# Attention heads taken in pairs, and rotary rows exchanged by transfers within SBUF

## The chip, the cores and the metric

The kernel runs on one core of a Trainium2 chip. The metric is the time of one execution in microseconds (us) on the device; of several executions the median is given. TensorE is written PE, its weight loads PEld, VectorE DVE, ScalarE ACT, GpSimd POOL and SyncE SP.

## The reference

Two transformer stacks of two layers each are applied to 256 positions of width 1024, in fp32. Most of the arithmetic is dense projections: feed-forward layers of hidden width 2816, input and output projections of the mixers, and a cross attention. Four self-attentions of eight heads of 64 stand among them. Cut to what the change touches:

```python
# A: forgetting attention      s = q @ k.T / 8 + cum_logf[q] - cum_logf[k], causal
# B: differential attention    4 heads of two maps each, rotary q and k, chunk mask:
#    p = softmax(s0) - lam * softmax(s1);  out = p @ v          (v is 128 wide)
# D: chunk band attention      s = q @ k.T / 8 + rel_table[clip(q - k)], chunk mask
# E: dilated attention         rotary q and k, log(count of patterns) as bias
rot = concat([x1 * cos - x2 * sin, x2 * cos + x1 * sin])   # x1, x2: dims 0..7 and 8..15 of a head
p = softmax(where(allowed, s, -inf));  out = p @ v
```

## The kernel before

All activations lie transposed: 128 features on the partitions, 256 positions along the row. A dense product is split into high and low fp32r parts (`hi*hi`, `lo*hi`, `hi*lo`), so one *unit* of weights (8 blocks of 128x128, or 4 for half of a row range) is 24 (or 12) matmuls of 128x256 on PE, lines 598, 599, 602 or 616 to 618. `plan_stream` lists all units in order. Weights come by SP into a ring of four buffers `raw`; ACT copies a unit to `w_hi` (line 984) and DVE subtracts to `w_lo` (line 1376), each when PE has finished the unit that held the slot before, up to four units ahead. PE, ACT, DVE and POOL each run the same written-out program `order`, in which every stage takes lists of units ("between") as filler, so that PE has dense work while the attention's softmax runs on ACT and DVE. `take` on PE is the matmuls of a unit, on ACT the split of a later unit into `w_hi`, on DVE the evacuation of the unit's PSUM bank (one of four, `acc`) and the split into `w_lo`.

One attention (`attend`) runs in 11 steps over 8 heads. In step i PE computes the scores of head i (lines 707, 708; contraction over 64 partitions; causal blocks only, so 384 columns in PSUM bank `wide[:, i % 2]`), turns the probabilities of head i-2 (line 717: three 128x128 transposes), multiplies head i-3 by its values (lines 727, 728; 64 output rows, the partition half of the head), and then takes the step's filler. DVE adds the bias and finds the row maximum (`biased`), and scales the probabilities of the head before (`probs`); ACT takes the exponential and its sum (line 1133) and copies the turned probabilities to SBUF (line 1141); DVE copies a finished pair of heads out (line 1625). fp32 matmuls are recorded as two passes each.

Ahead of B and E `rotate` forms, on PE, the rotary partner of every row by a permutation matrix (line 688, four matmuls of 128x512); DVE reads it from PSUM and makes `x*cos + partner*sin` by three instructions for each pair of blocks (lines 1574, 1576, 1577: a *spin*, four of them). The first two spins are needed for the first scores. Ahead of D `band_bias` reads the relative bias of each head by a skewed transfer, mirrors it by a reversal matrix on PE (line 824) and adds the mask on DVE (lines 1724, 1725). The same `rotate` with another matrix serves the retention after E, and is not changed.

Of the kernel before, what the change touches and what calls it, by code (L numbers as in the profile page):

```python
# [15 lines left out]
P = 128  # L16
# [36 lines left out]
class Counts:  # L53


    def __init__(self):
        self.norm = 0
        self.gen = 0
        self.fill = 0
        self.head = 0  # L60
        self.rot = 0
        self.att = 0
        self.pv = 0
        self.group = 0
        self.conv = 0
# [115 lines left out]
def build(nc, io, out):  # L181
# [22 lines left out]
    with ExitStack() as ctx:  # L204
# [24 lines left out]
        silu_g = sb("silu_g", [P, 2, T])  # L229
        hidf = sb("hidf", [P, 2, T])  # L230
# [8 lines left out]
        ident, ones, ones64, perm_rope, perm_ret = (mats[:, i, :] for i in range(5))  # L239
        reverse = mats[:, 6, :]  # L240
# [19 lines left out]
        rot_done, rot_added = sem("rot_done"), sem("rot_added")  # L260
# [23 lines left out]
        band_in, band_turned, band_masked = sem("band_in"), sem("band_turned"), sem("band_masked")  # L284
# [33 lines left out]
        def band(h):  # L318
            return work[:, 8 + 2 * h:10 + 2 * h, :] if h < 4 else keep[:, 8 + 2 * (h - 4):10 + 2 * (h - 4), :]
# [3 lines left out]
        def gate_bias(h):  # L323
            if h < 5:
                return flat(work[:, 8:16, :])[:, TRI * h:TRI * h + TRI]
            return flat(keep[:, 4:8, :])[:, TRI * (h - 5):TRI * (h - 4)] if h < 7 else lower(hidf)

        def slot_prob(g):
            return lower(prob[:, g % 3, :, :])

        def slot_turned(n):
            return lower(probT[:, n % 2, :, :])
# [5 lines left out]
        def attention(kind):  # L338

            def halves(v, b0):

                return [(h, [(v[:, :, 64 * h:64 * h + 64], 0, 64 * (h % 2))], [b0 + h // 2] if h % 2 else []) for h in range(8)]

            if kind == "A":
                return ([(half(16, h), half(20, h), gate_bias(h), None) for h in range(8)], halves(vals(32, 4), 0), 0.125)
            if kind == "B":
                v = vals(36, 4)
                return ([(half(24, i), half(28, i), chunked, i - 1 if i % 2 else None) for i in range(8)],  # L350
                        [(2 * h + 1, [(v[:, :, P * h:P * h + P], 0, 0)], [4 + h]) for h in range(4)], 0.125)
            if kind == "D":
                return ([(half(16, h), half(20, h), lower(band(h)), None) for h in range(8)], halves(vals(36, 4), 4), 0.125)
# [1690 lines left out]
```

## Time and profile before

| | |
|---|---|
| median of 3 executions | 2274.04 us (2272.51 to 2276.78) |
| the profiled execution | 2286.41 us, of which its span 2284.3 |
| PE busy | 2208.1 us (97%) |
| DVE busy | 1521.3 us (67%) |
| ACT busy | 1184.3 us (52%) |
| mean granted PE clock | 0.989 |

The span runs from the first to the last instruction. Busy time of PE is that of pipelined matmuls whose ends are modelled, so two records overlap and the distance between starts is what a matmul costs. The four attentions lie at 276 to 328 (A), 348 to 405 (B, with its rotation), 961 to 1024 (D, with its band) and 1492 to 1563 us (E, with its rotation).

### The profile page before, as it was taken

What the parts mean: (1) busy time and instruction counts of PE and PEld (TensorE: products, weight loads), DVE (VectorE), ACT (ScalarE), POOL (GpSimd) and SP (SyncE); (2) the same over time, 40 slices, a digit from 0 to 9 for tenths busy, and PEclk for the clock granted to TensorE, in tenths of its full rate; (3) what the DMA queues carried; (4) which work ended last, traced back from release to release, by engine and by line L of the source; (5) the groups of instructions that cost most, each with busy time, mean ns of one, the idle gap of its engine ahead of it and who ended that gap; (6) DMA issues with size and microseconds to landing.
All of it is one profiled execution on the core that took longest, in us unless ns stands there. A gap on an engine that the chain in (4) does not pass through costs nothing.

```text
span 2284.3 us, 45071 instructions
## 1 busy us (share of the span) xinstructions
PE 2208.1 (97%) x18355; PEld 2145.9 (94%) x18355; DVE 1521.3 (67%) x2344; ACT 1184.3 (52%) x1852; POOL 122.7 (5%) x146
## 2 busy tenths in 40 slices
PE   5999998899999999999999999999999999989998
PEld 5999987899999999888999999988999999989998
DVE  5766657676666666666766666677766666667664
ACT  5644453665456544446654554535654554556543
POOL 2001000110011001001100000100100000101001
PEclk9999998999999999999999999999999999999999
DMA  7555532356565657423665665642765665635653
GB/s 240 179 180 175 165 120 65 111 177 206 181 194 168 209 180 236 156 80 106 207 199 188 198 188 192 220 142 86 224 194 187 195 202 183 188 101 180 191 193 102
DMA packets 383756, 393.29 MB, mean 172 GB/s; under 512 B 6897, under 2 KB 381809, under 8 KB 383425
## 3 DMA queue, kind: packets, MB, share of 16 engines
q1 hardware_dynamic: 381632, 383.30, 52.7%
q0 software_dynamic: 1920, 7.11, 1.1%
q8 instruction: 148, 2.42, 0.5%
q14 instruction: 56, 0.45, 0.1%
HBM read 389.34 MB, written 1.05 MB: 171 GB/s over the span
## 4 chain that ended last, share of the span: by engine, by line
PE 86%; DVE 6%; ACT 4%; issue 2%; POOL 1%; DMA 1%; SPq 0%; POOLq 0%; DVEq 0%; ACTq 0%
PE acc L598 24%; PE acc L599 24%; PE acc L602 24%; DVE w_lo L1376 2%; ACT w_hi L984 2%; PE acc L616 2%; PE acc L617 2%; PE acc L618 2%; PE acc L567 1%; PE acc L569 1%; PE acc L568 1%; POOL t L1883 1%; PE wide L727 1%; DMA raw<-in_ffn_w_in 1%; PE wide L782 1%
## 5 line engine op out<-in xcount | busy, mean ns | idle before, releaser
L1376 DVE TENSOR_TENSOR w_lo<-raw,w_hi 128x1024 fp32r<-128x1024 f32 (+2 forms) x790 | 897.8, 1139 | 503.7 <-ACT w_hi L984 501.3
L984 ACT ACTIVATE w_hi<-raw 128x1024 fp32r<-128x1024 f32 (+2 forms) x790 | 776.3, 988 | 806.6 <-PE acc L602 739.4
L598 PE MATMUL acc<-hn_hi,w_hi 128*128 128x256 f32 x3328 | 792.7, 280 | 25.3 <-DMA colc<-in_cols 18.1
L599 PE MATMUL acc<-hn_lo,w_hi 128*128 128x256 f32 x3328 | 786.3, 278 | 0.0
L598 PEld LDWEIGHTS acc<-hn_hi,w_hi 128*128 128x128 f32 x3328 | 628.9, 189 | 30.6 <-DMA colc<-in_cols 18.1
L599 PEld LDWEIGHTS acc<-hn_lo,w_hi 128*128 128x128 f32 x3328 | 629.1, 189 | 0.9 <-issue 0.8
L602 PE MATMUL acc<-hn_hi,w_lo 128*128 128x256 f32 x3328 | 449.6, 278 | 0.0
L602 PEld LDWEIGHTS acc<-hn_hi,w_lo 128*128 128x128 f32 x3328 | 412.6, 188 | 0.0
L599 PE MATMUL acc<-hid_lo,w_hi 128*128 128x256 f32 x1408 | 331.6, 277 | 0.0
L598 PE MATMUL acc<-hid_hi,w_hi 128*128 128x256 f32 x1408 | 331.5, 277 | 0.0
L599 PEld LDWEIGHTS acc<-hid_lo,w_hi 128*128 128x128 f32 x1408 | 264.8, 188 | 0.0
L598 PEld LDWEIGHTS acc<-hid_hi,w_hi 128*128 128x128 f32 x1408 | 264.7, 188 | 0.0
L1883 POOL TENSOR_TENSOR t<-t 128x256 f32<-128x256 f32 x119 | 107.8, 906 | 2152.5 <-ACT t L1026 2105.8
L602 PE MATMUL acc<-hid_hi,w_lo 128*128 128x256 f32 x1408 | 192.4, 277 | 0.0
L602 PEld LDWEIGHTS acc<-hid_hi,w_lo 128*128 128x128 f32 x1408 | 175.2, 188 | 0.0
L598 PE MATMUL acc<-mn_hi,w_hi 128*128 128x256 f32 x512 | 132.6, 295 | 4.2 <-DVE mn_lo L1478 4.2
L599 PE MATMUL acc<-mn_lo,w_hi 128*128 128x256 f32 x512 | 126.9, 283 | 0.0
L598 PEld LDWEIGHTS acc<-mn_hi,w_hi 128*128 128x128 f32 x512 | 99.3, 194 | 7.7 <-issue 7.2
L1511 DVE TENSOR_TENSOR silu_g<-acc,rstd 128x256 f32<-128x256 f32 x176 | 74.4, 423 | 40.8 <-PE acc L602 28.0
L599 PEld LDWEIGHTS acc<-mn_lo,w_hi 128*128 128x128 f32 x512 | 99.3, 194 | 0.9 <-issue 0.7
L1520 DVE TENSOR_TENSOR hidf<-silu_g,acc 128x256 f32<-128x256 f32 x176 | 73.8, 420 | 28.7 <-PE acc L602 27.0
L1430 DVE SCALAR_TENSOR_TENSOR hn_lo<-x,gains,hn_hi 128x256 fp32r<-128x256 f32 x112 | 82.1, 738 | 8.9 <-ACT hn_hi L1022 8.9
(255 smaller groups left out, 2261.5 us busy)
## 6 DMA issues: line engine op xcount, KB each, us to landing
raw<-in_ffn_w_in SPq DMA_DIRECT2D x88, 1024.0 KB, 5.1
raw<-in_ffn_w_out SPq DMA_DIRECT2D x32, 1024.0 KB, 5.2
raw<-in_ffn_pre_w_gate SPq DMA_DIRECT2D x22, 1024.0 KB, 5.4
raw<-in_ffn_pre_w_up SPq DMA_DIRECT2D x22, 1024.0 KB, 5.3
raw<-in_ffn_post_w_gate SPq DMA_DIRECT2D x22, 1024.0 KB, 5.3
raw<-in_ffn_post_w_up SPq DMA_DIRECT2D x22, 1024.0 KB, 5.4
raw<-in_x_w_kv SPq DMA_DIRECT2D x16, 1024.0 KB, 5.5
raw<-in_ffn_pre_w_down SPq DMA_DIRECT2D x16, 1024.0 KB, 5.1
```

The costliest lines, as they stand in the source:

```text
L598: nc.tensor.matmul(bank, wh[:, j, :], a_hi[:, u.k0 + j, :], start=u.first and j == 0, stop=False)
L599: nc.tensor.matmul(bank, wh[:, j, :], a_lo[:, u.k0 + j, :], start=False, stop=False)
L602: mm = nc.tensor.matmul(bank, wl[:, j, :], a_hi[:, u.k0 + j, :], start=False, stop=u.last and j == u.nk - 1)
L616: nc.tensor.matmul(bank, ah, wh, start=j == 0, stop=False)
L617: nc.tensor.matmul(bank, ah, wl, start=False, stop=False)
L618: mm = nc.tensor.matmul(bank, al, wh, start=False, stop=j == u.nk - 1)
L984: nc.scalar.activation(w_hi[:, u.slot, 0:u.nk, :], raw[:, u.raw % RING, 0:u.nk, P * u.half:P * u.half + P], ACT.Copy).then_inc(w_hi_ready, 1)
L1376: nc.vector.tensor_tensor(w_lo[:, u.slot, 0:u.nk, :], raw[:, u.raw % RING, 0:u.nk, P * u.half:P * u.half + P], w_hi[:, u.slot, 0:u.nk, :]. ...
L1430: nc.vector.scalar_tensor_tensor(hn_lo[:, k, :], x[:, k, :], gains[:, gain + k:gain + k + 1], hn_hi[:, k, :].bitcast(F32), ALU.mult, ALU.s ...
L1511: nc.vector.tensor_tensor(silu_g[:, h, :], out_ap(units[u0 + h].out), rstd[:, 0, :], ALU.mult)\
L1520: nc.vector.tensor_tensor(hidf[:, h, :], silu_g[:, h, :], out_ap(units[u0 + 2 + h].out), ALU.mult).then_inc(hid_mul, 1)
L1883: nc.gpsimd.tensor_tensor(t1[:, 0, :], t1[:, 0, :], t1[:, k, :], ALU.add).then_inc(squares_added, 1)
```

## The change

Heads are taken two by two. `attend` has five steps instead of eleven. In step m, PE issues the first score matmul of both heads of pair m, then the second of both; head 0 lies on partitions 0 to 63, head 1 on 64 to 127, and their scores go to banks 0 and 1 of `wide`. Then follow filler, the transposes of head 0 of pair m-1, filler, the transposes of head 1, filler, and the values of both heads of pair m-1, which write partitions 0 to 63 and 64 to 127 of one bank. DVE makes one instruction for the bias of a pair (128x768) and two for its scaling; ACT's exponentials stay four for a pair. In B only the second of two maps is turned, and its values are 128 wide, so no two of them stand side by side there.

The permutation matmuls ahead of B and E go. ACT issues eight transfers (four of 8x1536 and four of 8x512 elements) that exchange rows 0 to 7 and 8 to 15 of each half into `prob` and `probT`, after its last split, and DVE's spins wait for all of them and read SBUF instead of PSUM; the sign is in the sine table. The band of D is laid out whole on the host, comes by two transfers instead of eight, and gets its mask by four DVE instructions of 128x768, which stand between the projections of D; line 824 goes. The deal of filler units over the steps is rewritten.

```diff
@@ order
-                    att("A", spread(memk[5:8] + span("bq", "bk")))
+                    att("A", deal(memk[5:8] + span("bq", "bk"), 1, 1, 1, 1, 1, 0, 1, 1, 0, 1, 1, 0, 1, 1, 0))
...
-                    rotate(work[:, 24:32, :], perm_rope, rope_c, rope_s, memv[2:4])
-                    att("B", [memv[4:6], memv[6:8], [(0, 4)], half[0:1], half[1:2], half[2:3], half[3:4], [], [], [], []])
-                    head(cat[:, 4:8, :], 4, 128, ["subln"] * 4, half[4:6], half[6:8])
+                    rope(work[:, 24:32, :], rope_c, rope_s, memv[2:4])
+                    att("B", [[memv[4:6], memv[6:8], [(0, 4)]], [half[0:1], half[1:2], []], [half[2:3], [], []],
+                              [half[3:4], [], []], [half[4:5], [], []]])
+                    head(cat[:, 4:8, :], 4, 128, ["subln"] * 4, half[5:6], half[6:8])
...
-                    att("D", [memv[0:2], memv[2:4], memv[4:6], memv[6:8] + [(0, 4)], half[0:1], half[1:2], half[2:3], half[3:4],
-                              half[4:5], half[5:6], half[6:8]], final=True)
+                    att("D", [[memv[0:2], memv[2:4], []], [memv[4:6], memv[6:8], [(0, 4)]], [half[0:1], half[1:2], half[2:3]],
+                              [half[3:4], half[4:5], half[5:6]], [half[6:7], half[7:8], []]], final=True)
...
-                    rotate(work[:, 28:36, :], perm_rope, dil_c, dil_sn, span("ev"))
-                    att("E", spread(span("rq", "rk", "rg")), final=True)
+                    rope(work[:, 28:36, :], dil_c, dil_sn, span("ev"))
+                    att("E", deal(span("rq", "rk", "rg"), 1, 1, 1, 1, 1, 0, 1, 1, 0, 1, 1, 0, 1, 1, 1), final=True)
@@ PE, attend
+                def score(m):
+                    if kind in "BE" and m < 2:
+                        pe.wait_ge(rot_added, c.rot - 2 + 2 * m)
+                    if m:
+                        pe.wait_ge(biased, c.att + 2 * m)
+                    for j, (q, k) in enumerate(heads(m)):
+                        nc.tensor.matmul(wide[:, j, 0:P], q[:, 0:P], k[:, 0:P], start=True, stop=True)
+                    for j, (q, k) in enumerate(heads(m)):
+                        nc.tensor.matmul(wide[:, j, P:TRI], q[:, P:T], k, start=True, stop=True).then_inc(scores, 1)
...
+                def weigh(m):
+                    vs = values(m)
+                    n, size = len(vs) * m, P // len(vs)
+                    pe.wait_ge(turned_copied, c.pv + n + len(vs))
...
+                for m in range(5):
+                    if m < 4:
+                        score(m)
+                    take(between[m][0])
+                    if m and kind != "B":
+                        turn(m - 1, 0, 2 * m - 2)
+                    take(between[m][1])
+                    if m and kind != "B":
+                        turn(m - 1, 1, 2 * m - 1)
+                    elif m:
+                        turn(m - 1, 1, m - 1)
+                    take(between[m][2])
+                    if m:
+                        weigh(m - 1)
@@ ACT, attend
+                for m in range(5):
+                    take(between[m][0])
+                    if m and kind != "B":
+                        copy_turned(2 * m - 2)
+                    if m < 4:
+                        exponent(m)
+                    take(between[m][1])
+                    if m:
+                        copy_turned(per * m - 1)
+                    take(between[m][2])
...
@@ ACT, rope
+                for b, home in ((0, rope_first), (6, rope_last)):
+                    for p0 in (0, 64):
+                        for to, at in ((p0, p0 + 8), (p0 + 8, p0)):
+                            act.dma_start(home[to:to + 8], src[at:at + 8, b:b + (2 if b else 6), :]).then_inc(rot_in, 16)
+                take(between)
@@ DVE, rope and attend
+                dve.wait_ge(rot_in, 128 * (c.rope + 1))
+                for b in (0, 2, 1, 3):
+                    home = rope_first[:, 2 * b:2 * b + 2, :] if b < 3 else rope_last
+                    spin(src[:, 2 * b:2 * b + 2, :], t1[:, 2 * b:2 * b + 2, :], home, cs, sn)
...
+                for m in range(5):
+                    if m and kind != "B":
+                        normalise(m - 1)
+                    if m < 4:
+                        bias(m)
+                    if m and kind == "B":
+                        normalise(m - 1)
+                    take(between[m][0])
+                    take(between[m][1])
+                    take(between[m][2])
+                    if m:
+                        copy_out(m - 1)
```

The order of the instructions shows the same in two places. The first is PE in the middle of A, from the end of one filler unit to the start of the next; before it reads

```order
L602 MATMUL acc<-hn_hi,w_lo 128x256 x8
L707 MATMUL wide<-work 128x128
L708 MATMUL wide<-work 128x256
L717 MATMUL wide<-mats,prob 128x128 x3
L727 MATMUL wide<-probT,work 64x256
L728 MATMUL wide<-probT,work 64x128
```

and of the changed kernel (line 620 is the end of a unit, 729 the transposes, 740 and 742 the values, 719 and 721 the scores)

```order
L620 MATMUL acc<-hn_hi,w_lo 128x256 x8
L729 MATMUL wide<-mats,prob 128x128 x3
L740 MATMUL wide<-probT,work 64x256 x2
L742 MATMUL wide<-probT,work 64x128 x2
L719 MATMUL wide<-work 128x128 x2
L721 MATMUL wide<-work 128x256 x2
```

Values and scores of two heads now stand together, and the values of a pair follow the transposes of its second head with no unit between. The second place is ACT in the same stretch, two steps of before and one of after (line 984, then 1002, is the split of a weight unit, 1133, then 1149, the exponential, 1141, then 1157, the copy of turned probabilities):

```order
L1133 ACTIVATE prob,small<-prob,small 128x128
L1133 ACTIVATE prob,small<-prob,small 128x256
L1141 ACTIVATE probT<-wide 128x384
L984 ACTIVATE w_hi<-raw 128x1024
L1133 ACTIVATE prob,small<-prob,small 128x128
L1133 ACTIVATE prob,small<-prob,small 128x256
L1141 ACTIVATE probT<-wide 128x384
L984 ACTIVATE w_hi<-raw 128x1024
```

```order
L1002 ACTIVATE w_hi<-raw 128x1024
L1157 ACTIVATE probT<-wide 128x384
L1149 ACTIVATE prob,small<-prob,small 128x128
L1149 ACTIVATE prob,small<-prob,small 128x256
L1149 ACTIVATE prob,small<-prob,small 128x128
L1149 ACTIVATE prob,small<-prob,small 128x256
L1002 ACTIVATE w_hi<-raw 128x1024
L1157 ACTIVATE probT<-wide 128x384
```

The copy that the values wait for stood ahead of the split, and stands behind it now.

## Rows read from the trace of the kernel before

**Rows 1.** Page, its heading and part 1: busy us, share of span, instructions.
```profile
span 2284.3 us, 45071 instructions
PE 2208.1 (97%) x18355; PEld 2145.9 (94%) x18355; DVE 1521.3 (67%) x2344; ACT 1184.3 (52%) x1852; POOL 122.7 (5%) x146
```
**Rows 2.** Stretches A, B, D, E: length, busy us by engine, clock, DMA share, GB/s.
```profile
276.40:328.10 51.70, 49.41 (x356) 41.52 (x356) 34.85 (x77) 22.11 (x51) 0.00 (x0) 1.00 0.41 123
348.00:404.50 56.50, 48.47 (x287) 41.23 (x286) 41.03 (x97) 20.81 (x54) 0.00 (x0) 0.82 0.21 66
961.20:1024.00 62.80, 58.65 (x395) 47.84 (x394) 42.23 (x109) 25.05 (x64) 0.00 (x0) 1.00 0.23 71
1492.40:1562.80 70.40, 67.27 (x483) 57.03 (x482) 50.31 (x102) 28.96 (x61) 0.00 (x0) 1.00 0.33 107
```
**Rows 3.** Timeline of PE around A: start us, us, line, operation, shape, count.
```profile
270.10 1.07 PE L602 MATMUL acc<-mn_hi,w_lo 128*128 128x256 f32 x8
272.82 1.07 PE L602 MATMUL acc<-mn_hi,w_lo 128*128 128x256 f32 x8
...
276.54 0.48 PE L707 MATMUL wide<-work 64*128 64x128 f32 x2
...
280.32 0.48 PE L707 MATMUL wide<-work 64*128 64x128 f32 x2
...
305.74 0.48 PE L707 MATMUL wide<-work 64*128 64x128 f32 x2
...
306.59 0.55 PE L717 MATMUL wide<-mats,prob 128*128 128x128 f32 x3
...
310.80 0.49 PE L707 MATMUL wide<-work 64*128 64x128 f32 x2
```
**Rows 4.** Timeline of PE in the last mixer: matmuls on halves of the array.
```profile
2016.11 1.98 PE L895 MATMUL wide<-work 128*64 128x64 f32 x32
...
2038.26 1.13 PE L909 MATMUL wide<-work,t 64*128 64x256 f32 x6
```
**Rows 5.** Timeline of ACT in A, split and copy behind one unit.
```profile
320.29 1.06 ACT L984 ACTIVATE w_hi<-raw 128x1024 fp32r<-128x1024 f32 x1 [2.83 <-PE acc L602]
321.26 0.47 ACT L1141 ACTIVATE probT<-wide 128x384 f32<-128x384 f32 x1
```
**Rows 6.** Groups of DVE by shape: count, busy us, mean ns, idle before.
```profile
L1376 DVE TENSOR_TENSOR w_lo<-raw,w_hi 128x768 fp32r<-128x768 f32 x64 | 61.2, 956 | 67.3 <-ACT w_hi L984 66.7
```
**Rows 7.** Timeline of PE at the band of D.
```profile
961.21 2.74 PE L824 MATMUL wide<-work,mats 128*128 128x384 f32 x8
...
968.07 0.48 PE L707 MATMUL wide<-work 64*128 64x128 f32 x2 [0.85 <-DVE keep L1725]
```
**Rows 8.** Timelines of PE, ACT and DVE at the rotation of B.
```profile
348.12 3.60 PE L688 MATMUL wide<-work,mats 128*128 128x512 f32 x8
...
357.29 0.49 PE L707 MATMUL wide<-work 64*128 64x128 f32 x2
...
348.38 2.00 ACT L984 ACTIVATE w_hi<-raw 128x1024 fp32r<-128x1024 f32 x2 [3.65 <-PE acc L618]
...
351.75 0.68 DVE L1574 TENSOR_TENSOR t<-wide,keep 128x512 f32<-128x512 f32 x1
...
353.67 0.68 DVE L1574 TENSOR_TENSOR t<-wide,keep 128x512 f32<-128x512 f32 x1
```
**Rows 9.** Timeline of DVE at the rotation of E.
```profile
1495.05 0.68 DVE L1574 TENSOR_TENSOR t<-wide,work 128x512 f32<-128x512 f32 x1
```
**Rows 10.** One issue on SP; then issues of transfers: KB each, us to landing.
```profile
2015.65 0.37 SPq L544 DMA_DIRECT2D raw<-in_gla_w_in  x1
...
keep<-in_band POOLq DMA_DIRECT2D x4, 256.0 KB, 9.5
out<-t SPq DMA_DIRECT2D x4, 256.0 KB, 2.1
```
**Rows 11.** Stretch in B: length, busy us by engine, clock, DMA share, GB/s.
```profile
370.00:380.00 10.00, 6.53 (x34) 5.15 (x32) 7.62 (x22) 5.24 (x16) 0.00 (x0) 0.67 0.16 54
```

More of the change, by code:

```diff
@@ L338, in attention, with heads, values @@
         def attention(kind):
[L342 to L353, printed above, removed]
-            return ([(half(28, h), half(32, h), dil_bias, None) for h in range(8)], halves(vals(40, 4), 0), 0.125)
+            q0, k0, bias, v, out0 = {"A": (16, 20, gate_pair, vals(32, 4), 0), "B": (24, 28, lambda m: both(chunked), vals(36, 4), 4),
+                                     "D": (16, 20, band_pair, vals(36, 4), 4), "E": (28, 32, lambda m: both(dil_bias), vals(40, 4), 0)}[kind]
+            def heads(m):
+                return [(half(q0, 2 * m + j), half(k0, 2 * m + j)) for j in range(2)]
+            def values(m):
+                return [v[:, :, P * m:P * m + P]] if kind == "B" else [v[:, :, P * m + 64 * j:P * m + 64 * j + 64] for j in range(2)]
+            return heads, bias, values, out0
         def order(s):
@@ L816, in gate_biases @@
                         mm.then_inc(gates_spread, 1)
-            def band_bias(c):
-                pe.wait_ge(band_in, 16 * 9)
-                pe.wait_ge(head_std, c.head)
-                for h in range(8):
-                    if h >= 4:
-                        pe.wait_ge(band_masked, h - 3)
-                    nc.tensor.matmul(wide[:, h % 4, 0:TRI], reverse, lower(band(h)), start=True, stop=True)\
-                        .then_inc(band_turned, 1)
-                pe.wait_ge(band_masked, 8)
             def retention(c, half):
@@ L1562, in head_norm, with spin @@
                 take(after)
[L1564 to L1568 removed]
+            def spin(pair, turned_pair, shifted, cs, sn):
+                nc.vector.tensor_tensor(turned_pair, shifted, sn.to_broadcast([P, 2, T]), ALU.mult)
+                link(nc.vector.tensor_tensor(pair, pair, cs.to_broadcast([P, 2, T]), ALU.mult))
+                nc.vector.tensor_tensor(pair, pair, turned_pair, ALU.add).then_inc(rot_added, 1)
@@ L1911, in residual @@
                     pool.dma_start(work[:, 40:42, :], io["masks"][:, 2:4, :]).then_inc(band_in, 16)
-                    for h in range(8):
-                        b = io["band"]
-                        skew = bass.AP(b.tensor, 512 * h, [[1, P], [P, 2], [1, T]])
-                        pool.dma_start(band(h), skew).then_inc(band_in, 16)
+                    pool.dma_start(work[:, 8:14, :], io["band"][:, 0:6, :]).then_inc(band_in, 16)
+                    pool.dma_start(keep[:, 8:14, :], io["band"][:, 6:12, :]).then_inc(band_in, 16)
                 if name == "down4":
```

322 lines of the change are left out of this document (150 added, 172 removed).

## The prediction

> **What bounds the kernel now.** I read the page's busy times first, then the four stretches that hold the attentions, then the order of time inside them. PE is busy for 97% of the span [rows 1]; it runs its program in order, so a microsecond of PE work that goes is a microsecond of time, unless PE then waits. In A, D and E PE is busy 49.4 of 51.7, 58.7 of 62.8 and 67.3 of 70.4 us at full clock; DVE has 35 to 50 us there and ACT 22 to 29 [rows 2]. B is different: PE has 48.5 of 56.5 us at a mean clock of 0.82, DVE 41.2 [rows 2]; it waits on a chain of short instructions, and its clock falls to half where PE has run thin (6.5 of 10 us busy, 0.67 granted, [rows 11]). So the change is worth PE time in A, D and E, and chain length in B.
>
> **What a head costs PE.** A unit of 24 matmuls is 2.72 us (272.82 - 270.10, [rows 3]); a half unit 1.36. Scores alone cost 280.32 - 276.54 - 2.72 = 1.06. Scores, transposes and values of one step cost 310.80 - 305.74 - 2.72 = 2.34 [rows 3], so a pair costs 4.7.
>
> **What a pair will cost PE.** Do two halves of the array run side by side? Line 909 has three matmuls of 64 rows, the first two on different halves, six passes. It ends after 1.13 us [rows 4]; a pass of 256 columns is 2 cycles a column, 0.21 us by my estimate from two unit matmuls of 0.113 (2.72/24), so six in a row with a tail of 0.4 would be 1.5 and four 1.1. So row halves run together. For column halves line 895 doesn't decide: 32 passes of 64 columns in 1.98 us [rows 4] are 0.05 to 0.06 each, which 32 in a row would also give. For the values of a pair I bound: 1.0 us (together) to 1.7 (in a row); I take 1.1. With both together a pair costs one step of a head, 2.34, and a second set of transposes, at most 0.55 [rows 3], 0.45 taken: 2.8 instead of 4.7, so 1.9 less for each of 12 pairs in A, D and E.
>
> The Trainium skill (TensorE: Matmul & The Clock Gate, part 3 on packing small matmuls) gives 3.07 times for four row tiles and 2.38 times for three column tiles, not four and three. An estimate from that page for two tiles is 1.6 times: 0.25 us more on each of 16 score pairs and 12 value pairs, 7 us, and the sum below would be 13 instead of 20.
>
> **The new wait.** In A and E most steps have two units and nothing between the second transposes and the values. Before, ACT copied a head turned in one step for values in the next. Now the copy comes behind the split of the second unit: the row of before has the copy done 1.44 after the split began (321.26 + 0.47 - 320.29, [rows 5]); with an estimated 0.25 from a unit's end to ACT's start that is 1.69 after the unit. The transposes take 0.35 of that, so PE waits 1.35 a pair. Queued behind the values are the scores of the next pair, so all wait. A step of A is then 2 x 2.72 + 2.34 + 0.45 + 1.35 = 9.6, against 2 x 5.06 = 10.1. Does DVE keep up? The bias of a pair is 768 columns, 0.96 by a subtraction of that width [rows 6], or 1.25 ns a column; the maxima of 256 and 512 add 1.0; scaling a pair is 1.2 by the same rate. Three times 1.6 for units and their evacuation make it 5.8 to 7.4 in a step, less than 9.6. ACT has four exponentials (1.8), two copies and two splits, 4.8.
>
> **A.** First step 1.06 + 3 x 2.72 = 9.2; three of 9.6; last without scores 8.6; together 46.6. Before, 276.5 to 328.1 [rows 2, 3]. Less 0.4 for the columns: gain 4.5.
>
> **D.** The band goes: 968.07 - 961.21 = 6.9 us of PE and wait [rows 7]. Its four DVE masks of 768 (1 us each, by [rows 6]) lie between projections, whose unit of 2.72 asks DVE for 1.6; nothing is late there as PE has units split ahead. First step 1.06 + 4 units = 11.9; the second 2.0 + 10.9 + 0.8 + a wait of 1.4 = 15.2. In the third and fourth PE has 7.0 only, and DVE sets the pace: copy out, high and low part of the pair before (1.5), scaling 1.2, bias 2.0, then ACT's exponentials, split and copy 2.9, the values 1.0: 9.0 and 8.4. Last 6.8, and 0.6 for the last block's low part. Together 51.9 against 62.8 [rows 2]: gain 10.9, less 0.4.
>
> **B and its rotation.** Before, ACT ended its split at 350.4 (348.38 + 2.0), DVE began the spins at 351.75, two spins (1.92 each) later PE scored at 357.29 [rows 8]; meanwhile PE had 3.6 us of rotation and two units. Now ACT must issue eight transfers. An issue on SP lasts 0.37 [rows 10], so eight take 3.0; the landing I take as 2.1, as for the smallest load of the listed rows. Nothing in the trace goes from SBUF to SBUF or is issued by ACT: bounds 1 us (everything hidden behind DVE's own split) and 9.5 + 8 x 0.7 = 15, that of the band's transfers on POOL [rows 10] (an issue estimated at twice SP's). I take 5.1, as both are plain hardware transfers. Spins start at 355.4, 3.7 later; scores at 359.3, 2.0 later than before, with PE idle for 5.8 us since it has no rotation. A hole of 3.5 us has lowered the clock here before [rows 11], so I charge 3 more. Against it the chain: a pair is one bias, one maximum, one scaling where two stood, 6.5 us a step instead of two of 4.3, and one unit fewer stands behind it: 6 saved. Net gain 1, between -4 and +6.
>
> The Trainium skill (DMA: Bandwidth & Descriptors, where the 2 us goes) puts the sequencer's dispatch at about 50 ns. By that eight issues would be 0.4, not 3.0, the spins 2.6 earlier in B and E, and the sum 25. The trace's 0.37 stands against it for SP; no row has ACT.
>
> **E.** Spins start 3.8 later than 1495.05 [rows 9]: 1498.8. Four spins 7.7, then four evacuations and splits of 1.55, then bias 2.0: 1514.7. PE has done its four units long before, waits for a bank until 1507, and comes to its second scores at 1515.3. The step after it is 12.6, since DVE holds three units' work ahead of the scaling; two of 9.6; the last 10.0; 0.7 until the last pair is copied: 1557.8 against 1562.8 [rows 2]. Gain 5.0, less 0.4.
>
> **Sum.** 4.5 + 10.5 + 1 + 4.6 = 20.6; say 20. It comes off the profiled execution's 2286.4 (span 2284.3, [rows 1]): 2266. That execution lies 12 above the median of 2274.0; taken off the median: 2254.
>
> **Rivals.**
> 1. *The waits don't come*: copies and transfers hide. Then all PE work counts: 12 x 1.9 = 22.8, four score pairs in B 4.2, band 6.9, two rotations about 3.4 each: 40.7, so 2233. For it: PE is 97% busy [rows 1]. Against it: the copy has 1.35 us behind a split that can't start earlier, and PE has nothing between.
> 2. *The exchange is late*, 10 us instead of 5. B and E each lose 5, and the longer hole costs B 2.5 more at half clock: gain 8, so 2266. For it: one semaphore counts eight transfers and weight loads use the same engines.
> 3. *Halves run in turn.* The change then doesn't do what it says: a score pair costs 1.7 (+0.64 x 16), a value pair 1.7 (+0.6 x 12): 17 less, gain 3: 2271. Against it: line 909 for rows; the columns are open.
> 4. *Slower*: the exchange takes over 15 us from its first issue, as POOL's transfers of the band would. Every microsecond beyond 5 is paid in B and in E, as PE has but two units (B) and four banks (E) to work on meanwhile. Break-even is 5 + 20/2 = 15; at 17 it is 2278.
>
> **How the numbers follow.** Forecast 0.58 (its own range 2246 to 2262), rival 1 0.15, rival 2 0.15, rival 3 0.07, rival 4 0.05. Below 2238 lies half of rival 1, above 2268 rivals 3 and 4: left out about 0.2, so 2238 to 2268. What a measurement can tell from no change is 0.2%, 4.5 us. Faster than 2269.5: forecast, rival 1, rival 2 but for a small part, 0.87; same 0.08; slower 0.05.
>
> **What would show it.** Right: in the changed trace the two score matmuls of a pair start within a few hundredths of a microsecond; the values wait for ACT's copy some 1.3 us in most steps of A and E; PE idles 5 to 6 us ahead of B's first scores with the transfers as releaser; no reversal in D. Wrong: if that hole is under 2 us, the issues are cheap and rival 1 gains; if the second value matmul starts a pass later than the first, the columns run in turn; if DVE's evacuations hold PE in A, my step there is too short. The forecast fails if the exchange takes over 10 us or if D, the largest term, gains under 6.

## The result, and the profile after

Two timings of the changed kernel are on record, each beside runs of the kernel before.

| timing | changed kernel, median (runs) | kernel before, median (runs) | ratio, 95% interval |
|---|---|---|---|
| first | 2266.32 us (7: 2255.11 to 2273.31) | 2276.78 us (7: 2272.51 to 2285.90) | 0.995 [0.9927, 0.9972] |
| second, the same kernel again | 2263.07 us (6: 2259.30 to 2268.36) | 2279.82 us (11: 2275.99 to 2285.60) | 0.9925 [0.9909, 0.9941] |

The change is faster, by 10.5 us in the first timing and 16.8 in the second; forecast were 2254 and a gain of 20. The time lies in the outer range (2238 to 2268), though above the forecast's own (2246 to 2262); the direction is right, the size is short. The page of the changed kernel, its heading and its first part [rows 1]:

```profile
span 2253.3 us, 44894 instructions
PE 2153.0 (96%) x18323; PEld 2110.6 (94%) x18323; DVE 1512.0 (67%) x2244; ACT 1183.1 (53%) x1852; POOL 117.5 (5%) x140
```

The two profiled executions differ by 31.0 us of span, PE's busy time by 55. That is more than either timing gives, so the stages have to be read apart. Below is each attention with what stands around it, of before and then of after: from the first matmul of the head norm ahead of it (D, A), or from the norm of the residual ahead of the projections (E), to the first landmark behind it that both kernels share (A and B: the next head norm; D: the cross attention; E: the first retention scores). Columns as in [rows 2]: stretch, length, busy us of PE, PEld, DVE, ACT, POOL, granted clock, DMA share, GB/s.

```profile
264.80:333.35 68.55, 66.26 (x482) 56.45 (x481) 43.38 (x92) 33.23 (x59) 0.00 (x0) 1.00 0.43 128
333.35:404.50 71.15, 63.12 (x390) 53.97 (x389) 50.52 (x113) 29.99 (x61) 0.00 (x0) 0.86 0.21 69
946.85:1042.05 95.20, 89.65 (x642) 76.76 (x641) 66.43 (x150) 48.11 (x97) 5.93 (x7) 1.00 0.35 113
1475.30:1577.25 101.95, 98.78 (x736) 86.58 (x735) 73.34 (x136) 44.86 (x89) 0.05 (x1) 1.00 0.41 135
```

```profile
258.90:322.50 63.60, 58.31 (x483) 52.58 (x482) 41.60 (x68) 32.70 (x59) 0.00 (x0) 1.00 0.48 148
322.50:392.45 69.95, 53.68 (x382) 47.50 (x381) 48.91 (x98) 29.80 (x62) 0.00 (x0) 0.93 0.21 65
927.00:1012.10 85.10, 76.27 (x626) 69.71 (x625) 59.90 (x110) 47.72 (x97) 5.94 (x7) 1.00 0.39 125
1444.10:1546.20 102.10, 88.81 (x728) 82.50 (x728) 71.67 (x112) 44.65 (x89) 0.06 (x1) 0.97 0.43 139
```

A, B and D became 4.95, 1.2 and 10.1 us shorter (forecast 4.5, 1 and 10.5). E became 0.15 longer, where 4.6 were forecast: PE has 10 us less to do in it and idles for all of them. The four together are 16.1 us.

Most of the other 15 us between the two profiles does not come from the change. A unit of 24 dense matmuls takes either 2.72 or 2.83 us, at a granted clock of 1.00 in both. In the execution of before, the feed-forward after the first norm (some 86 to 260 us) and the one from 711 to 935 us run at the slower pace; in that of after, neither does. The last matmul group of two units in a row, PE's timeline of before, then of after:

```profile
122.17 1.11 PE L602 MATMUL acc<-hn_hi,w_lo 128*128 128x256 f32 x8
125.00 1.11 PE L602 MATMUL acc<-hn_hi,w_lo 128*128 128x256 f32 x8
```

```profile
120.85 1.07 PE L620 MATMUL acc<-hn_hi,w_lo 128*128 128x256 f32 x8
123.57 1.07 PE L620 MATMUL acc<-hn_hi,w_lo 128*128 128x256 f32 x8
```

The starts are 2.83 apart in the one and 2.72 in the other. Over the 14 profiles of this case (both kernels and twelve runs below) the first of these stretches is slow in eight and the second in nine, whichever kernel runs; five other dense stretches that I sampled never are. They account for 4.7 and some 7 us of the 31. If timed runs change pace in the same way, that is up to 12 of the 18 us between the fastest and the slowest run of the first timing.

Now E. The rows are the end of the split on ACT and the issues (ACTq is ACT's queue, the second number the time of all four issues), the first rotation on DVE, and on PE the first scores, the unit behind them, the second scores and the first work behind the attention:

```profile
1461.64 1.06 ACT L1002 ACTIVATE w_hi<-raw 128x1024 fp32r<-128x1024 f32 x1 [1.66 <-PE acc L620]
1462.09 2.84 ACTq L1308 DMA_DIRECT2D prob<-work  x4
1464.96 2.61 ACTq L1308 DMA_DIRECT2D probT<-work  x4
```

```profile
1471.97 0.69 DVE L1604 TENSOR_TENSOR t<-prob,work 128x512 f32<-128x512 f32 x1 [8.01 <-DMA probT<-work]
```

```profile
1476.07 0.51 PE L719 MATMUL wide<-work 64*128 64x128 f32 x4 [3.65 <-DVE work L1606]
...
1480.23 0.58 PE L616 MATMUL acc<-hn_hi,w_hi 128*128 128x256 f32 x1 [2.80 <-DVE work L1452]
...
1490.00 0.49 PE L719 MATMUL wide<-work 64*128 64x128 f32 x4
...
1531.44 3.67 PE L706 MATMUL wide<-work,mats 128*128 128x512 f32 x8 [2.09 <-DVE keep L1659]
```

Eight issues take 5.5 us, 0.65 to 0.71 each; DVE goes on 4.4 us after the end of the last (1471.97 - 1467.57). From its first issue the exchange takes 1471.97 - 1462.09 = 9.9 us (9.3 from the end of the split, 1462.70). In B it takes 345.50 - 337.66 = 7.8 from its first issue, of which 2.0 lie behind the last, and there PE waits 6.55 for the first scores:

```profile
337.66 1.23 ACTq L1308 DMA_DIRECT2D prob<-work  x1
...
338.91 1.96 ACTq L1308 DMA_DIRECT2D prob<-work  x3
340.90 2.61 ACTq L1308 DMA_DIRECT2D probT<-work  x4
```

```profile
345.50 0.69 DVE L1604 TENSOR_TENSOR t<-prob,keep 128x512 f32<-128x512 f32 x1 [4.56 <-DMA probT<-work]
```

```profile
349.60 0.80 PE L719 MATMUL wide<-work 64*128 64x128 f32 x4 [6.55 <-DVE work L1606]
```

The hole in E lowers the clock as well. PE stands still for 3.65 and for 2.80 us, and from 1476.4 to 1483.2 the granted clock is 0.50, the lower of its two levels (1.2 GHz). The matmuls of the first unit in it start 0.213 us apart and not 0.113, which costs some 1.3 us. In all seven profiles with eight transfers the clock falls at this place, for 6.8 us (10.2 in one); in the seven others it does not fall there.

Last, a step of A, on PE and on ACT: after the first two pairs' scores, the step's second unit ends with L620, and the values (L740, L742) and scores (L719, L721) of a pair stand behind the second transposes (L729).

```profile
270.61 0.49 PE L719 MATMUL wide<-work 64*128 64x128 f32 x4
...
279.83 0.49 PE L719 MATMUL wide<-work 64*128 64x128 f32 x4
...
295.31 1.08 PE L620 MATMUL acc<-hn_hi,w_lo 128*128 128x256 f32 x8
296.22 0.49 PE L729 MATMUL wide<-mats,prob 128*128 128x128 f32 x3
297.97 0.65 PE L740 MATMUL wide<-probT,work 128*64 128x256 f32 x4 [1.26 <-ACT probT L1157]
298.45 0.39 PE L742 MATMUL wide<-probT,work 128*64 128x128 f32 x4
298.77 0.49 PE L719 MATMUL wide<-work 64*128 64x128 f32 x4
```

```profile
296.49 1.05 ACT L1002 ACTIVATE w_hi<-raw 128x1024 fp32r<-128x1024 f32 x1
297.44 0.47 ACT L1157 ACTIVATE probT<-wide 128x384 f32<-128x384 f32 x1
```

PE waits 1.26 us for a copy that stands behind a split, as [rows 5] let expect. The starts of the first two pairs' scores in A are 279.83 - 270.61 = 9.22 apart, with three units of 2.72 between, so the scores of a pair take 1.06. The values of a pair take 298.77 - 297.97 = 0.80 us for eight passes; the two matmuls that stand on different halves start 0.007 us apart, for values (column halves) as for scores (row halves).

### The profile page after: what moved, and what is told of

The parts are those of the page before. It is cut to its first block, busy times and chain, and to the rows that moved or that the text cites. A ratio compares the mean times of both kernels' runs of the same rounds, so it can differ in the third digit from the quotient of the medians.

```text
span 2253.3 us, 44894 instructions
## 1 busy us (share of the span) xinstructions
PE 2153.0 (96%) x18323; PEld 2110.6 (94%) x18323; DVE 1512.0 (67%) x2244; ACT 1183.1 (53%) x1852; POOL 117.5 (5%) x140
## 4 chain that ended last, share of the span: by engine, by line
PE 82%; DVE 7%; ACT 5%; issue 3%; DMA 1%; POOL 1%; ACTq 0%; SPq 0%; POOLq 0%; DVEq 0%
PE acc L616 24%; PE acc L620 23%; PE acc L617 23%; DVE w_lo L1415 2%; ACT w_hi L1002 2%; PE acc L634 2%; PE acc L636 1%; PE acc L635 1%; PE acc L585 1%; PE acc L587 1%; PE acc L586 1%; POOL t L1932 1%; ACT prob L1149 1%; DMA raw<-in_ffn_w_in 1%; DVE hn_lo L1469 1%
## 5 line engine op out<-in xcount | busy, mean ns | idle before, releaser
L620 PE MATMUL acc<-hn_hi,w_lo 128*128 128x256 f32 x3328 | 447.3, 277 | 0.0
L620 PEld LDWEIGHTS acc<-hn_hi,w_lo 128*128 128x128 f32 x3328 | 410.5, 188 | 0.0
L620 PE MATMUL acc<-hid_hi,w_lo 128*128 128x256 f32 x1408 | 190.9, 276 | 0.0
L620 PEld LDWEIGHTS acc<-hid_hi,w_lo 128*128 128x128 f32 x1408 | 173.9, 188 | 0.0
L1550 DVE TENSOR_TENSOR gates_hid<-acc,rstd 128x256 f32<-128x256 f32 x176 | 74.4, 423 | 38.5 <-PE acc L620 27.0
L1559 DVE TENSOR_TENSOR gates_hid<-gates_hid,acc 128x256 f32<-128x256 f32 x176 | 73.9, 420 | 26.7 <-PE acc L620 26.1
```

Source lines behind the costliest of these rows:

```text
L620: mm = nc.tensor.matmul(bank, wl[:, j, :], a_hi[:, u.k0 + j, :], start=False, stop=u.last and j == u.nk - 1)
L1550: nc.vector.tensor_tensor(silu_g[:, h, :], out_ap(units[u0 + h].out), rstd[:, 0, :], ALU.mult)\
L1559: nc.vector.tensor_tensor(hidf[:, h, :], silu_g[:, h, :], out_ap(units[u0 + 2 + h].out), ALU.mult).then_inc(hid_mul, 1)
```

## The experiments

**Theory:** the pairs and the band bring what was worked out (16 us in A, B and D); E lost its gain to an exchange that takes 9 us and not 5; what the first timing lacks beside that is the pace of the dense stretches. **Rivals:** E lost it to the pairs themselves (DVE's wider operations); or the change brings only the 10.5 us of the first timing, and something outside the attentions takes the rest. A third shows in the traces, the clock: where the mean granted clock of a stage differs between two runs, its length is no measure of waits alone, and this is said below where it matters.

Stage lengths of all profiles, by the same landmarks (us), and the timed ratios to before:

| kernel | A | B | D | E | ratio, 95% interval |
|---|---|---|---|---|---|
| before | 68.5 | 71.1 | 95.2 | 101.9 | |
| changed | 63.6 | 70.0 | 85.1 | 102.1 | 0.995 [0.9927, 0.9972] |
| changed, again | 63.7 | 70.0 | 85.2 | 101.7 | 0.9925 [0.9909, 0.9941] |
| permutation matmuls | 63.7 | 67.9 | 85.0 | 99.1 | 0.9894 [0.9878, 0.9911] |
| copy before split | 60.5 | 73.7 | 86.6 | 102.0 | 0.9911 [0.9893, 0.9929] |
| two semaphores | 63.7 | 71.4 | 85.0 | 100.1 | 0.9923 [0.9901, 0.9944] |
| unit behind each turn | 70.4 | 70.0 | 84.2 | 107.0 | 0.9993 [0.9975, 1.0012] |
| the same, permutation matmuls | 70.6 | 68.1 | 84.3 | 101.5 | 0.9939 [0.9918, 0.9961] |
| band alone | 68.7 | 70.9 | 88.4 | 103.2 | 0.9944 [0.9926, 0.9961] |
| exchange alone | 68.5 | 77.4 | 95.2 | 108.3 | 1.0043 [1.0024, 1.0062] |
| two transfers | 63.7 | 66.3 | 85.1 | 97.1 | 0.9873 [0.9843, 0.9904] |
| scaling between units | 63.3 | 70.0 | 83.8 | 103.9 | 0.994 [0.9916, 0.9963] |
| all together | 61.7 | 68.4 | 83.8 | 97.4 | 0.9876 [0.9842, 0.9909] |
| split before exponentials | 59.4 | 67.3 | 83.8 | 94.3 | 0.987 [0.9844, 0.9896] |

### The changed kernel again

> The changed kernel once more, unaltered. Theory: its trace gains 5.0 us in A, 1.2 in B, 10.1 in D and loses 0.2 in E, 16 in all; the rest of the 31 us between the two profiled executions is dense stretches in which a unit of before took 2.83 us instead of 2.72, at the same granted clock, which come and go. Then the ratio to before is near 0.993 (0.991 to 0.995) and the landmarks of the attentions come out within 0.5 us of the first profile. Rival: the change really gains 10.5 as the first timing says, 0.9953, and some stage outside the attentions loses 5.

0.9925, and every stage within 0.5 us of the first profile. The stages' 16 us (0.993) lie inside this interval, and at the edge of the first. The rival's 0.9953 lies outside the second. The mean of the two timings, some 14 us, is the best single figure for the change.

### Permutation matmuls for both embeddings

```
             def rope(c, src, cs, sn, between):    # PE
-                take(between)
+                rotate(c, src, cs, sn, between, perm_rope)
             def rope(c, src, cs, sn, between):    # ACT
-                ... eight act.dma_start(home[...], src[...]).then_inc(rot_in, 16)
                 take(between)
             def rope(c, src, cs, sn, between):    # DVE
-                dve.wait_ge(rot_in, 128 * (c.rope + 1))
+                dve.wait_ge(rot_done, c.rot + n + 1)   # per pair, from PSUM
```

> Pairs of heads and the laid-out band stay; both rotary embeddings get their rows by permutation matmuls again. Theory (the exchange is what was mis-sized): the spins of E start 8 us earlier after the stage begins, those of B 4.6 earlier, PE has 3.5 us more of work in each; E becomes 5 to 7 us shorter than in the changed kernel, B 3 to 5, in all 8 to 12, so some 2256 where the changed kernel has 2266. Rival (E lost its gain to the pairs themselves, for instance to DVE's wider operations): E stays within 2 us of the changed kernel and the total moves by less than 3.

2257.1 us against 2263.1 for the changed kernel beside it: 6 us, where 8 to 12 were expected. E is 2.5 to 3 shorter (expected 5 to 7), B 2.1 (3 to 5). So the exchange costs more than the matmuls that it replaced; the rival is out. PE gets its 3.5 to 4.2 us of rotation back, and in this run it does not wait ahead of E's scores at all: the 8 us by which the spins come earlier are worth only what PE had lost there, 3.65 and 2.80 us of waits and 1.3 by the clock. In this run the clock is at half for 3.4 us near the end of E, which the changed kernel's is not.

### Two of eight transfers

```
-                    for p0 in (0, 64):
-                        for to, at in ((p0, p0 + 8), (p0 + 8, p0)):
+                    for p0 in (0,):
+                        for to, at in ((p0, p0 + 8),):
-                dve.wait_ge(rot_in, 128 * (c.rope + 1))
+                dve.wait_ge(rot_in, 32 * (c.rope + 1))
```

> The changed kernel with two of the eight transfers of the exchange, one from each half; six are left out, so that three of four groups of rows are rotated with what the buffers held before, and the output is another. It measures what the count of issues costs. Theory (0.7 us of ACT's queue for each issue, and the landing behind the last): the spins start 4 us earlier in B and E; E is 3.5 to 4.5 us shorter than in the changed kernel, which is what the prediction missed in E, and B 1 to 4 shorter as its clock goes. Rival (landing behind the weights' transfers sets the end): the spins start less than 1.5 us earlier and E keeps its length.

This is the cleanest test of the failed term. DVE's first spin of E and the issues ahead of it:

```profile
1464.77 0.66 ACTq L1308 DMA_DIRECT2D prob<-work  x1
1465.46 0.82 ACTq L1308 DMA_DIRECT2D probT<-work  x1
```

```profile
1467.98 0.69 DVE L1604 TENSOR_TENSOR t<-prob,work 128x512 f32<-128x512 f32 x1 [1.33 <-DMA probT<-work]
```

From the first issue to the spins it is 3.2 us here and 9.9 in the changed kernel: 1.5 of issues and 1.7 of landing in place of 5.5 and 4.4. What sets the landing stays open: with the same eight queued it was 2.0 to 2.2 in B and 4.0 to 5.0 in E over three profiles, so the count alone doesn't, and the weights' transfers as a cause were not tested apart. Counted from the stage's start the spins of E come 6.7 us earlier than in the changed kernel (expected 4). E is 97.1, 4.9 below before (forecast 4.6), and B 66.3; the total is 0.9873. These 3.2 us are 1.9 less than the 5.1 that I had assumed, so the run shows that the exchange is what E lost by, but not that 5.1 would have given the whole 4.6.

### A semaphore of its own for the last four transfers

```
-    src[at:at + 8, b:b + (2 if b else 6), :]).then_inc(rot_in, 16)
+    src[at:at + 8, b:b + (2 if b else 6), :]).then_inc(rot_in_last if b else rot_in, 16)
-    dve.wait_ge(rot_in, 128 * (c.rope + 1))
+    dve.wait_ge(rot_in, 64 * (c.rope + 1))
+    ... if b == 3: dve.wait_ge(rot_in_last, 64 * (c.rope + 1))
```

> The first four transfers of the exchange (six of eight blocks) count on a semaphore of their own, so the first three spins need not wait for the last four transfers. Theory (eight issues of 0.7 us in a row on ACT are the larger part of the 8 to 9 us): spins start 2.5 to 4 us earlier in B and in E, and each ends 2 to 3 earlier: 4 to 6 us faster than the changed kernel. Rival (the transfers land late and together, since they share the DMA engines with the weights): spins start less than 1 us earlier and the total stays.

DVE's wait for the transfers falls from 8.01 to 5.77 us in E and from 4.56 to 2.44 in B, 2.2 earlier, a little short of expected. E is 1.5 to 2 shorter, a little less than expected. In B PE's wait ahead of the first scores falls from 6.6 to 4.4, but the stage is 1.4 longer, at a mean clock of 0.86 instead of 0.93; the total doesn't move (0.9923). The theory holds for the spins and for E; that the clock took B's gain is argued from its mean alone.

### The exchange alone, on the kernel before

```
-    rotate(work[:, 24:32, :], perm_rope, rope_c, rope_s, memv[2:4])
+    rope(work[:, 24:32, :], rope_c, rope_s, memv[2:4])
-    rotate(work[:, 28:36, :], perm_rope, dil_c, dil_sn, span("ev"))
+    rope(work[:, 28:36, :], dil_c, dil_sn, span("ev"))
```

> The kernel before with one part of the change: rows for both rotary embeddings exchanged by eight transfers on ACT's queue, heads one by one, the band reversed on PE (and 1 us of clearing buffers on DVE at the start). Theory (the exchange takes 8 to 9 us and DVE's spins start 4.6 and 8 us later): B 2 to 6 longer, E 1 to 5 longer, the total 3 to 9 slower than before. Rival (PE's 7 us of rotation count in full): 4 to 7 faster.

1.0043: 9.8 us slower. B is 6.3 and E 6.4 longer, all three a little above what was expected, and more than in the pairs' kernel. B's mean clock is 0.80 here and was 0.86 before; that heads one by one leave less slack as well is not shown.

### The band alone, on the kernel before

```
-    s.band_bias(c)                       # 8 reversals on PE, 16 additions on DVE
+    project("cb", "cc"); s.band_bias(range(0, 2)); project("ch"); s.band_bias(range(2, 4))
```

> The kernel before with one part of the change: the band of D laid out in memory, masked by four additions on DVE between projections; heads one by one, permutation matmuls. Theory: the 6.9 us of reversal leave PE and nothing takes their place; D from 95.2 to 88.3 and the total 6 to 7 faster than before (0.997). So of the 10.1 that D gains in the changed kernel, 3 are due to the pairs. Rival: the masks delay the projections or D's heads wait for DVE instead: gain under 3.

```profile
939.00:1027.45 88.45, 84.13 (x626) 73.95 (x625) 62.14 (x134) 48.14 (x97) 5.93 (x7) 1.00 0.37 120
```

D is 88.45, by 6.75 shorter, as its 6.9 on PE [rows 7] let expect; 3.35 of D's 10.1 are the pairs'. The timed 12.5 is more than D explains, and more than the 6 to 7 expected. In the profiled execution the second of the two dense stretches is a quick one for most of its length; that this makes the difference in the timed runs is not shown.

### The copy ahead of the split

```
                     if m < 4:
                         exponent(m)
-                    take(between[m][1])
                     if m:
                         copy_turned(per * m - 1)
+                    take(between[m][1])
```

> ACT copies the second turned head of a pair before it splits the weights behind the unit in the middle, not after. Theory (the wait of 1.26 us ahead of the values is the copy queued behind that split): the wait falls to about 0.6, as in B where nothing is queued ahead; with four such waits in A, four in D and four in E, 0.6 each, 5 to 7 us faster than the changed kernel. Rival (the wait is the latency of transposes to copy to values, whatever ACT does): 1.2 stays. Second rival: the split that now comes 0.8 later makes PE wait for weights; same or slower.

PE's waits in the whole program, of after and of this run (us in total, times, longest):

```profile
PE wide L740 <- ACT probT L1157: 16.3, 15, 1.5
```

```profile
PE wide L740 <- ACT probT L1157: 8.6, 15, 0.6
```

The wait is the queue's on ACT: it fell to 0.6 as expected, and A by 3.1. But D became 1.5 longer, in part since PE now waits for DVE's scaling there (4.7 us in place of 2.5). E kept its length: its waits for the copy fell from 4.0 to 1.7 us, but its clock was at half for 10.2 us in place of 6.8. B became 3.7 longer. B's own waits hardly changed; its clock did. Two stretches of 10 us in B's steps, of after, then of this run:

```profile
371.00:381.00 10.00, 6.41 (x45) 4.72 (x44) 7.05 (x17) 4.16 (x14) 0.00 (x0) 1.00 0.18 54
381.00:391.00 10.00, 5.99 (x43) 5.01 (x42) 7.41 (x21) 3.99 (x12) 0.00 (x0) 1.00 0.17 54
```

```profile
373.00:383.00 10.00, 6.33 (x36) 4.75 (x38) 7.26 (x18) 4.52 (x16) 0.00 (x0) 0.91 0.17 54
383.00:393.00 10.00, 7.46 (x37) 6.03 (x36) 6.34 (x19) 2.87 (x10) 0.00 (x0) 0.67 0.17 52
```

PE runs about as thin in the one as in the other and is at full clock in the one only. The total, 0.9911, isn't told apart from the changed kernel's 0.9925; 5 to 7 us were expected.

### A unit behind each of the transposes

```
-    att("A", deal(memk[5:8] + span("bq", "bk"), 1, 1, 1, 1, 1, 0, 1, 1, 0, 1, 1, 0, 1, 1, 0))
+    att("A", deal(memk[5:8] + span("bq", "bk"), 1, 1, 1, 0, 1, 1, 0, 1, 1, 0, 1, 1, 0, 1, 1))
     # E in the same way; on DVE the scaling of pair m now ends step m, ahead of the copy out
```

> The changed kernel with another deal of units in A and E: from the second step on the first transposes stand right behind the scores, and the two units stand behind the first and the second transposes, so that ACT's copy for the values runs beside the second unit. On DVE the scaling of a pair comes before the copy out of the pair before it (also in D), else the first transposes would wait for it. Theory (PE waits because nothing stands between transposes and values): the waits of 1.26 us go in A and E, four in each, less a wait of up to 0.5 at the first transposes; A 4 to 5 us shorter than in the changed kernel, E 2 to 4, D 0 to 3; 7 to 11 faster than the changed kernel. Rival (DVE sets the pace of the step of 9.3 us anyway): PE waits as long for the transposes instead, the total moves by less than 3.

Wrong by its sign: A is 6.8 longer than in the changed kernel, E 5. In A the waits changed their place:

```profile
PE wide L729 <- DVE prob L1646: 9.5, 4, 2.8
```

```profile
298.77 0.17 DVE L1643 RECIPROCAL small<-small 128x4 f32<-128x4 f32 x1
298.98 1.03 DVE L1646 TENSOR_TENSOR prob<-prob,small 128x256 f32<-128x256 f32 x2
```

The first group is PE's waits in A, the second DVE's timeline: the scaling starts only behind the evacuation and split of the step's second unit, and PE's first transposes, which now come right behind the scores, wait for it. The waits are 4.2 us more than the changed kernel's 5.3. The rest of the 6.8 goes with the clock, which is at half for 3.4 us twice in this A (mean 0.95) and never in the changed kernel's. The rival had the place of the wait right, but not the size.

> The permutation matmuls of the run before and the new deal together. Theory: both gains add up, since one lies ahead of the attentions and the other inside them: 12 to 17 us faster than the changed kernel, some 2248 to 2252, ratio to before near 0.987. Rival: E is set by DVE's spins and backlog, so the two gains in E are one; 8 to 11 faster.

With the permutation matmuls beside it the same deal gives 0.9939: A as bad, E 5.5 better than with the exchange. A has the same two spells at half clock. Neither theory nor rival allowed for the loss in A.

### The scaling between the units

```
                     take(between[m][1])
+                    if m < 4 and kind != "B":
+                        normalise(m)
                     take(between[m][2])
-                    if m < 4 and kind != "B":
-                        normalise(m)
```

> The deal of the run with a unit behind each of the transposes, with DVE's scaling of a pair between the two units of its step and not behind both. Theory (there PE waited 2 to 2.8 us for a scaling queued behind the second unit's evacuation and split): the scaling is now done 2 us before the next pair's scores, both waits are gone, A is 58 to 60 us (63.6 in the changed kernel), E 3 to 5 shorter, D about 1 shorter: 8 to 11 faster than the changed kernel. Rival (DVE has no slack left in a step of 8 us, so the wait moves to the units or to the next scores): A stays over 62.

A is 63.3, over 62 as the rival had it, but not for the rival's reason alone. PE's waits in A fell from 9.5 to 3.7 us (2.4 for the scaling, 1.3 for the copy), and no wait for a unit stands in their place. The clock is at half for 3.4 us in this A. The next run has the same program in A and the same 3.7 us of waits, and is at full clock. The stretch of A, of this run and then of the next:

```profile
262.70:326.05 63.35, 59.59 (x483) 53.84 (x482) 40.83 (x68) 33.13 (x59) 0.00 (x0) 0.97 0.47 145
```

```profile
263.60:325.30 61.70, 57.94 (x483) 52.18 (x482) 40.59 (x68) 33.13 (x59) 0.00 (x0) 1.00 0.48 148
```

So the deal and the scaling are worth 1.9 us of A at full clock, and the clock took them back here. E, 103.9, is no shorter either; its clock is at half for 13.7 us. What is left of the waits comes from DVE, which idles 2.46 us for ACT's split of a unit's weights, and that stands behind four exponentials:

```profile
288.57 0.41 ACT L1149 ACTIVATE prob<-prob,small 128x128 f32<-128x128 f32 x1 [2.29 <-DVE small L1638]
...
290.34 1.04 ACT L1002 ACTIVATE w_hi<-raw 128x1024 fp32r<-128x1024 f32 x1
```

```profile
291.42 1.23 DVE L1415 TENSOR_TENSOR w_lo<-raw,w_hi 128x1024 fp32r<-128x1024 f32 x1 [2.46 <-ACT w_hi L1002]
```

### All together, and the split ahead of the exponentials

The first of these two is the deal and the scaling of the run above with the permutation matmuls.

> Pairs and the laid-out band, the rows by permutation matmuls, and the new deal with the scaling between the units. Theory: A 58 to 60, B 68, D 84.3, E 94 to 96: 27 to 32 us faster than before, ratio near 0.987, and 8 or more faster than the run with permutation matmuls alone. Rival (E is set by DVE): E stays at 99, ratio 0.989.

A 61.7, B 68.4, E 97.4; ratio 0.9876 (three runs; a fourth, of 6327 us, is left out). A and E miss what was expected by 1.4 us or more. The total is 28 us faster than before, as expected, but by the ratios only 4 faster than with the permutation matmuls alone, where 8 were expected; the rival is out. The second adds this on ACT, for A and E from the second step on:

```
+                    if early:
+                        take(between[m][1])
                     if m < 4:
                         exponent(m)
-                    take(between[m][1])
+                    if not early:
+                        take(between[m][1])
```

> The run with all together, and from the second step of A and E on ACT splits the weights behind the first unit before it does the pair's four exponentials, not after. Theory (in that run the chain of a step goes from DVE's maxima to ACT's exponentials, then ACT's split, for which DVE waits 2.5 us before it can do the low parts and the scaling): the split now comes 1.8 us earlier, DVE scales a pair 1 us earlier, PE's waits at transposes and values go; A 59 to 60.5 (61.7 before), E 95 to 96.5 (97.4), 2 to 4 us faster than the run with all together, ratio near 0.986. Rival (the exponentials, now 1 us later, hold the scaling just as long): A and E stay within 0.7.

```profile
263.40:322.80 59.40, 58.10 (x482) 52.48 (x481) 41.26 (x68) 33.20 (x59) 0.00 (x0) 1.00 0.49 154
1440.20:1534.55 94.35, 90.71 (x737) 82.94 (x736) 71.43 (x112) 44.67 (x89) 0.03 (x1) 1.00 0.44 147
```

PE is busy for 58.1 of A's 59.4 us; its waits in A for copy and scaling are 0.6 and 0.6, where the changed kernel has 5.3. This version, 2246.61 us (6 runs, 2243.18 to 2252.24), is faster than both kernels: 31 us less than the 2277.84 of before beside it, and by the ratios to before (0.987 and 0.9925) some 12 less than the changed kernel, which was timed on another chip. From the run with all together it is told apart by its stages (A 2.3, E 3.0 shorter), and not by the total (0.987 and 0.9876).

## Why the prediction was right or wrong

**What bounds the kernel: right.** In A PE's busy time and its one wait (58.3 and 5.3 us) make up the stage's 63.6, and B went by its chain.

**What a pair costs PE: right.** A pair's scores take 1.06 us, as one head's did [rows 3], and its values 0.80, less than the 1.0 that I had as the least: both kinds of halves run side by side, at twice the rate. Rival 3 is out, and so is the factor of 1.6 that I estimated from the Trainium skill (TensorE: Matmul & The Clock Gate, part 3 on packing small matmuls), which would have left a gain of 13: the trace disagrees with that estimate, which went from four and three tiles to two.

**The new wait: right in size and cause.** Forecast 1.35, measured 1.26, and the copy ahead of the split takes half of it away. Nearly all of it could be taken away in A (1.2 us of 5.3 were left), but only by moving three things at once; the first attempt moved it to DVE's scaling, and the second left 3.7.

**A and D: right; B: in part by luck.** 4.95 and 10.1 against 4.5 and 10.5; the band alone gave 6.75 of D. In B PE idled 6.55 us where 5.8 were forecast, and fell to half clock there. Its 1.2 meet the 1 forecast, but the terms do not: the first scores came 3.2 us later than before (forecast 2.0), and behind them 4.4 were saved, where I had 6 for the chain less 3 for the clock. The clock's mean over the stage rose, from 0.86 to 0.93, so that charge did not come; how much the chain alone saved is not shown.

**E, and the exchange: this is the step that failed.** "I take 5.1", eight issues at the 0.37 of SP and a landing of 2.1 [rows 10]. From its first issue the exchange took 9.9 us in E and 7.8 in B. The issues on ACT's queue took 5.5 and 5.9 where 3.0 were taken, 0.65 to 0.71 each in E; the landing behind the last was 4.4 in E, and only in B, at 2.0, the one that I had. Counted from the start of the stage, E's spins came 4.4 us later than forecast (27.9 for 23.5), its second scores 5.9 later (45.9 for 40.0) and the end of the attention 4.8 later (87.3 for 82.5). So the shortfall lies ahead of the second scores, and the steps behind them went as forecast or a little better. The second term there is the clock: the prediction had PE idle in E too, but charged the clock in B alone, and E paid some 1.3 us for it.

The upper bound of 15 held the exchange, the value taken didn't; rival 2 put 10 us at a chance of 0.15, and E lost 4.8 us by it, the 5 that this rival gave for E. That its total, 2266, is the first timing's is luck: it has B 7.5 worse, and B came out as forecast. The run with two transfers shows the term by itself: with 3.2 us E gains 4.9. The Trainium skill (DMA: Bandwidth & Descriptors, where the 2 us goes) puts a sequencer's dispatch at about 50 ns, in its account of transfers that GpSimd issues, which would have made the exchange shorter than I took it; the trace has 0.65 and more for each issue on ACT, so that figure can't stand for an issue there.

**The sum.** 16.1 us instead of 20.6 in the stages. The first timing's 10.5 lies lower still, the second's 16.8 does not; that the pace of two dense stretches makes this difference fits all profiles, but timed runs have no profile each, so it is argued and not shown. Outside A, B, D and E and those two stretches no stage of the two profiles differs by more than 2 us.

## What to carry to other kernels

A transfer that replaces work of the bound engine has to be costed from its first issue to its last landing with the issues in a row, and measured on the queue that issues it: eight small ones were 7.8 and 9.9 us here, where the matmuls that they replaced were 3.5 to 4.2. Where engines hand a step round (PE, DVE, ACT and back), taking one wait away can move it to the next queue; read each engine's order for what stands ahead of the piece that is waited for, and move all of them before judging the idea. Compare profiles stage by stage, between landmarks that the change doesn't touch, before a difference of spans is put down to the change, and read each stage's granted clock before its length is put down to waits.

## What the runs showed of the hardware

- Dense matmuls ran at one of two paces, 2.720 or 2.827 us for 24, at the same granted clock, for 170 to 220 us at a time, in two of seven stretches sampled, in 17 of 28 cases there. ACT and DVE took the same time for the same instruction in both (splits of 1.06 and 1.22 us). What sets it stays open.
- ACT's queue took 0.64 to 0.82 us for each issue of a small transfer within SBUF, with 1.2 for the first of B. The landing behind the last of eight was 2.0 to 2.2 us in B and 4.0 to 5.0 in E.
- Two matmuls on halves of the array, rows or columns, started 0.007 us apart and took the time of one (1.06 us for one head's scores and for two).
- In B, where PE is busy for about 6 of 10 us, the clock was at 1.00 through two such stretches in one run and at 0.67 in one of the other's, in the same steps. B was 1.4 and 3.7 us longer in two runs in which its mean clock was 0.86 and not 0.93.
- Behind a hole of 3.65 us on PE in E, the clock was at 0.50 for 6.8 us, and dense matmuls started 0.213 us apart in place of 0.113.
